# An expert layer's last turns reordered, and its results summed by selection products

## What is computed

```
logits = x @ w_router + b_router                 # 512 x 32
top_val, top_idx = top_k(logits, 4); gate = softmax(top_val)
for each token and each of its 4 experts e:
    hb = x @ w_e1[e] + b_e1[e]                   # 1024 -> 2048
    y += gate * (clamped_swiglu(hb) @ w_e2[e] + b_e2[e])   # 1024 -> 1024
out = layer_norm(DEEPNORM_ALPHA * x + y, ln2_g, ln2_b)
```

## Time and profile before

| | us |
|---|---|
| median of three runs | 1627.82 |
| the profiled execution | 1628.22 |
| its span | 1626.5 |
| TensorE busy | 1445.0 |
| VectorE busy | 605.8 |
| GpSimd busy | 348.2 |
| ScalarE busy | 141.2 |

### The profile page before, as it was taken

How to read it: one execution, slowest core, us unless ns; L and a number is a source line. 1 busy time by engine, 2 the same in 40 slices (tenths; PEclk the granted TensorE clock), 3 DMA queues, 4 the chain that set the end, 5 groups by cost and what they waited for, 6 DMA issues and landing times.

```text
span 1626.5 us, 28900 instructions
## 1 busy us (share of the span) xinstructions
PE 1445.0 (89%) x12008; PEld 638.0 (39%) x12009; DVE 605.8 (37%) x1048; ACT 141.2 (9%) x227; POOL 348.2 (21%) x390
## 2 busy tenths in 40 slices
PE   7999999999999979989977687897789999999855
PEld 6744444444444633333322232332233333344222
DVE  5034344210003645434433533443443354344326
ACT  4011322110000010000000000000000000000001
POOL 1060000000000022422332332332232233223225
PEclk9999999999999989999999999999999999999987
DMA  5522200163114389999999999999999999999936
GB/s 187 183 73 72 60 1 0 46 193 91 46 45 168 131 314 381 420 423 424 422 422 425 421 422 422 424 420 424 424 421 422 424 423 422 422 400 425 424 146 253
DMA packets 94327, 474.32 MB, mean 292 GB/s; under 512 B 15022, under 2 KB 60854, under 8 KB 68696
## 3 DMA queue, kind: packets, MB, share of 16 engines
q1 hardware_dynamic: 79520, 445.09, 67.8%
q0 software_dynamic: 12240, 16.86, 2.9%
q10 hardware_dynamic: 2536, 11.94, 1.9%
HBM read 469.59 MB, written 20.97 MB: 302 GB/s over the span
## 4 chain that ended last, share of the span: by engine, by line
PE 61%; DMA 31%; DVE 3%; issue 2%; ACT 1%; POOL 1%; SPq 0%; DVEq 0%; POOLq 0%
DMA big<-in_w_e 30%; PE ps L1543 19%; PE ps L1569 10%; PE ps L1397 7%; PE ps L1318 5%; PE ps L1279 4%; PE ps L1427 3%; PE ps L1455 3%; PE ps L1411 3%; PE ps L1405 1%; PE ps L1346 1%; PE ps L1364 1%; PE ps L1634 0%; DMA rest<-x_rows,P 0%; PE ps L1471 0%
## 5 line engine op out<-in xcount | busy, mean ns | idle before, releaser
L1543 PE MATMUL ps<-big,rest 128*32 128x512 f32 x5056 | 568.2, 599 | 95.8 <-DMA big<-in_w_e 82.2
L1543 PEld LDWEIGHTS ps<-big,rest 128*32 128x32 f32 x5056 | 159.9, 110 | 490.7 <-issue 490.4
L1569 PE MATMUL ps<-big,rest 128*32 128x256 f32 x5120 | 289.7, 383 | 32.1 <-DMA big<-in_w_e 30.9
L1569 PEld LDWEIGHTS ps<-big,rest 128*32 128x32 f32 x5120 | 167.0, 111 | 164.7 <-issue 42.8
L1155 DVE MEMSET stat<- 128x1 f32 x31 | 1.8, 59 | 493.0 <-PE ps L1543 493.0
L614 POOL DMA_INDIRECT rest<-x_rows,idx x124 | 152.4, 1229 | 58.3 <-issue 31.9
L626 POOL DMA_INDIRECT expert_rows<-rest,slot x128 | 126.9, 992 | 62.3 <-issue 34.1
L798 ACT ACTIVATE rest<-rest 128x1024 f32<-128x1024 f32 x32 | 33.9, 1060 | 924.6 <-DVE rest L1139 924.6
L610 POOL COPY idx<-P 128x4 uint32 (+1 forms) x31 | 5.8, 188 | 475.7 <-DVE rest L1156 468.1
L1318 PE MATMUL ps<-big,rest 128*128 128x512 f32 x192 | 84.4, 601 | 2.8 <-ACT big L676 2.8
L1156 DVE STREAM_TRANSPOSE rest<-rest 128x1024 f32<-128x1024 f32 x31 | 64.3, 2073 | 18.2 <-issue 18.2
(11 more groups left out here) (236 smaller groups left out, 1091.2 us busy)
## 6 DMA issues: line engine op xcount, KB each, us to landing
big<-in_w_e SPq DMA_DIRECT2D x190, 2048.0 KB, 25.5
rest<-in_w_in SPq DMA_DIRECT2D x14, 1024.0 KB, 5.2
big<-expert_rows ACTq DMA_DIRECT2D x8, 1024.0 KB, 12.1
gate_area<-in_w_in SPq DMA_DIRECT2D x8, 512.0 KB, 5.4
rest<-in_w_in SPq DMA_DIRECT2D x8, 512.0 KB, 4.7
big<-in_w_out SPq DMA_DIRECT2D x1, 4096.0 KB, 13.0
X<-in_x SPq DMA_DIRECT2D x4, 512.0 KB, 9.0
gate_area<-in_w_branch_mlstm SPq DMA_DIRECT2D x4, 512.0 KB, 6.3
```

The lines of the kernel that those rows point to most:

```text
L1543: last = mm(ps[TB * g:TB * (g + 1), b, :], xT[:, k, b, :], w1, start=(k == 0), stop=(k == KD - 1))
L1569: last = mm(ps[TB * g:TB * (g + 1), 4 + b // 2, YW * (b % 2):YW * (b % 2 + 1)], acts[:, k, b, :], W2[:, k, YW * g:YW * (g + 1)], start=(fi ...
```

## The change

SP, TensorE and VectorE end with fc2(31) ahead of fc1(32), and SP loads W2(31) ahead of W1(32). The rows of turns 1 to 31 are read back by SP's queue, in four loads of 2 MB and with 32 tokens x 4 choices on the 128 partitions, each into the place of one pair of W1. Those of turn 32 are not written to HBM: they stay in SBUF, are moved into one piece (`yL`, 16 copies of 32x256 on VectorE and ScalarE) and are added by a product with `slot_gate`, a matrix (row by token) that holds each row's gate where row and token belong together. Its row of gates is fetched by an indirect DMA from a copy of the gates in HBM (`gates`), and the places of these rows in `expert_rows` are set to zero at the start. The four choices of 32 tokens are summed by one product with `row_gate` (128 rows by 32 tokens); the gates for it come by a second copy in HBM (`main_gates`, zero for rows of turn 32), read back transposed (`main_rows`). The residual enters the sums by a product with the identity. The closing norm reads PSUM; GpSimd's and ScalarE's steps over rows are gone from it, and each tile is stored in two halves. `gates_of_late_rows` stands where the diagonals were made, and `late_selections` behind `turn_a(2)`, ahead of VectorE's loop.

```diff
+    gates_dram = nc.dram_tensor("gates", (S, TOPK), F32, kind="Internal").ap()
+    main_dram = nc.dram_tensor("main_gates", (S, TOPK), F32, kind="Internal").ap()
+    gate_of_row = gates_dram.rearrange("t (k a) -> (t k) a", a=1)
+    y_rows = y_dram.rearrange("t k n -> (t k) n")
...
+QROWS = TB * TOPK
+NQ = S // TB
+assert QROWS == P and NQ * D <= W1_COLS and 2 * FF * KD == NT * 4 * FF
+yg = cut(big, 0, NQ, D)
+row_gate = cut(gate_area, 0, NQ, TB)
+slot_gate = gate_area[:, 4 * S:5 * S]
+yL = cut(rest, SPARE_AT + KF * CAP, CG, YW)
...
-    with sp.Fori(1, n_it - 1) as it:
+    with sp.Fori(1, n_it - 2) as it:
         load_w1(it + 1, sp.snap((it + 1) % E))
         load_w2(it, sp.snap(it % E))
+    load_w2(n_it - 2, E - 2)
+    load_w1(n_it - 1, E - 1)
     load_w2(n_it - 1, E - 1)
+    sp.wait_ge(last_zeroed, 16 * NB)
+    sp.wait_ge(y_stored, n_it * (16 * NB) - 16 * NB)
     for i in range(NT):
-        sp.wait_ge(out_ready, i + 1)
-        sp.dma_start(out_rows[P * i:P * (i + 1), :], X0v[:, i, :]).then_inc(out_stored, 16)
-    sp.wait_ge(out_stored, 16 * NT)
+        sp.wait_ge(w1_used, n_it * PAIRS + (i + 1 - PAIRS))
+        sp.dma_start(yg[:, NT * i:NT * (i + 1), :],
+                     y_rows[TOPK * P * i:TOPK * P * (i + 1), :].rearrange("(j p) n -> p j n", p=P)).then_inc(yg_landed[i], 16)
+    for i in range(NT):
+        for n in range(D // BANK):
+            sp.wait_ge(out_ready, 2 * i + n + 1)
+            sp.dma_start(out_rows[P * i:P * (i + 1), BANK * n:BANK * (n + 1)], X0v[:, i, BANK * n:BANK * (n + 1)]).then_inc(out_stored, 16)
+    sp.wait_ge(out_stored, 32 * NT)
...
+    nc.gpsimd.tensor_copy(last_slot, slot_table[:, bass.ds(n_it * NB - NB, NB)]).then_inc(last_slots, 1)
+    pool.wait_ge(last_slots, 1)
+    own_wait()
+    for b in range(NB):
+        pool.indirect_dma_start(out=y_quarters, out_offset=bass.IndirectOffsetOnAxis(ap=last_slot[:, b:b + 1], axis=0),
+                                in_=no_rows, in_offset=None,
+                                bounds_check=S * TOPK * CG - 1, oob_is_err=False).then_inc(last_zeroed, 16)
+    pool.wait_ge(late_consts, 1)
+    pool.wait_ge(last_rows, 1)
+    pool.wait_ge(gates_stored, 32)
+    pool.indirect_dma_start(out=last_gate, out_offset=None, in_=gate_of_row,
+                            in_offset=bass.IndirectOffsetOnAxis(ap=last_row, axis=0),
+                            bounds_check=S * TOPK - 1, oob_is_err=False).then_inc(last_gates, 16)
...
     scatter(n_it - 1)
-    scatter(n_it)
-    pool.wait_ge(x1_scaled, 1)
-    pool.wait_ge(diags_ready, TOPK * NT)
-    def add_first(i):
-        pool.wait_ge(yg_front[i], 16)
-        row = yg[:, i, 0, :]
-        step(nc.gpsimd.tensor_scalar(row, row, gatew[:, TOPK * i:TOPK * i + 1], None, ALU.mult))
-        nc.gpsimd.tensor_tensor(X0v[:, i, :], X0v[:, i, :], row, ALU.add).then_inc(first_added, 1)
-    for i in range(NT):
-        add_first(i)
...
+    act.wait_ge(gates_ready, 1)
+    act.dma_start(gates_dram.rearrange("(i p) k -> p i k", p=P), cut(gatew, 0, NT, TOPK)).then_inc(gates_stored, 16)
+    act.dma_start(main_dram.rearrange("(i p) k -> p i k", p=P), cut(main_gate, 0, NT, TOPK)).then_inc(gates_stored, 16)
     act.wait_ge(x1_stored, 16 * NT)
     act.activation(X0[:], X0[:], ACT.Copy, scale=DEEP_ALPHA).then_inc(x1_scaled, 1)
+    act.wait_ge(gates_stored, 32)
+    act.dma_start(main_rows.rearrange("p (j a) -> p j a", a=1),
+                  main_dram.rearrange("(j t) (k a) -> (t k) j a", t=TB, a=1), allow_slow_non_contiguous=True).then_inc(main_landed, 16)
...
-    act.wait_ge(w2_used, n_it * W2_UNITS)
-    act.wait_ge(y_stored, n_it * (16 * NB))
-    for i in range(NT):
-        act.dma_start(yg[:, i, 0:2], y_dram[P * i:P * (i + 1), 0:2]).then_inc(yg_front[i], 16)
-        act.dma_start(yg[:, i, 2:4], y_dram[P * i:P * (i + 1), 2:4]).then_inc(yg_back[i], 16)
+    act.wait_ge(y_ready, n_it + 1)
+    for g in range(2, CG):
+        for b in range(NB):
+            act.activation(yL[TB * b:TB * (b + 1), g, :], yS[TB * g:TB * (g + 1), b, :], ACT.Copy).then_inc(late_moved, 1)
...
-        if i >= 1:
-            act.wait_ge(centred, i)
-            act.activation(X0v[:, i - 1, :], X0v[:, i - 1, :], ACT.Copy, scale=stat[:, s0 - 2:s0 - 1]).then_inc(scaled, 1)
...
+    def gates_of_late_rows():
+        step(nc.vector.tensor_scalar(last_round, cnt[:, E:E + 1], 1.0 / CAP, 0.5 * (CAP - 1) / CAP - 1.0, ALU.mult, ALU.add))
+        step(nc.vector.tensor_scalar(last_iter, last_round, float(E), float(E - 1), ALU.mult, ALU.add))
+        step(nc.vector.tensor_scalar(main_gate, itern[:], last_iter, None, ALU.not_equal))
+        nc.vector.tensor_tensor(main_gate, main_gate, gatew[:], ALU.mult).then_inc(gates_ready, 1)
+        dve.wait_ge(last_slots, 1)
...
+    def late_selections():
+        dve.wait_ge(late_consts, 1)
+        dve.wait_ge(main_landed, 16)
+        for j in range(NQ):
+            nc.vector.tensor_scalar(row_gate[:, j, :], fourth, main_rows[:, j:j + 1], None, ALU.mult).then_inc(row_gates, 1)
+        dve.wait_ge(last_rows, 1)
+        dve.wait_ge(last_gates, 16)
+        nc.vector.tensor_scalar(slot_gate, token_row, last_token, last_gate, ALU.is_equal, ALU.mult).then_inc(slot_gates, 1)
+    def move_late_rows(g):
+        for b in range(NB):
+            nc.vector.tensor_copy(yL[TB * b:TB * (b + 1), g, :], yS[TB * g:TB * (g + 1), b, :]).then_inc(late_moved, 1)
...
     turn_a(1)
-    for n in range(TOPK * NT):
-        i, k = n // TOPK, n % TOPK
-        nc.vector.tensor_scalar(gate_diag[:, n, :], ident[:], gw[:, i, k:k + 1], None, ALU.mult).then_inc(diags_ready, 1)
+    gates_of_late_rows()
     spread_b2(1)
     spread_b1(2)
     turn_x(3)
     swiglu(2)
     take_y(1, first=True)
     turn_a(2)
+    late_selections()
     with dve.Fori(2, n_it - 1) as it:
         spread_b1(it + 1)
         turn_x(it + 2)
...
         spread_b2(it)
         take_y(it)
         turn_a(it + 1)
+    spread_b2(n_it - 1)
+    take_y(n_it - 1)
     spread_b1(n_it)
     swiglu(n_it)
     turn_a(n_it, into=last_aT)
-    spread_b2(n_it - 1)
-    take_y(n_it - 1)
     spread_b2(n_it)
     take_y(n_it)
+    dve.wait_ge(y_ready, n_it + 1)
+    move_late_rows(0)
+    move_late_rows(1)
...
+    def norm_2_center(i):
         s0 = 16 * i
-        dve.wait_ge(first_added, i + 1)
+        b = SUM_AT[i]
+        dve.wait_ge(combined, i + 1)
         for n in range(D // BANK):
-            dve.wait_ge(combined, 2 * i + n + 1)
-            half = t[:, BANK * n:BANK * (n + 1)]
-            nc.vector.tensor_tensor(half, half, ps[:, 2 * i + n, :], ALU.add).then_inc(combined_read, 1)
-            dve.wait_ge(combined_read, 2 * i + n + 1)
-            piece_statistics(NORM2 + i, n, half)
+            piece_statistics(NORM2 + i, n, ps[:, b + n, :])
         step(nc.vector.bn_aggr(stat[:, s0 + 12:s0 + 14], stat[:, s0:s0 + 12]))
         nc.vector.tensor_scalar(stat[:, s0 + 13:s0 + 14], stat[:, s0 + 13:s0 + 14], LN_EPS, None, ALU.add).then_inc(var2_ready, 1)
-        layer_norm_center(NORM2 + i, t)
+        step(nc.vector.scalar_tensor_tensor(out=X0v[:, i, :], in0=ps[:, b:b + 2, :].rearrange("p b n -> p (b n)"),
+                                            scalar=stat[:, s0 + 12:s0 + 13], in1=gain[:], op0=ALU.subtract, op1=ALU.mult))
     def norm_2_root(i):
...
         step(nc.vector.scalar_tensor_tensor(out=q, in0=y, scalar=var, in1=y, op0=ALU.mult, op1=ALU.mult))
         step(nc.vector.tensor_scalar(q, q, -0.5, 1.5, ALU.mult, ALU.add))
         nc.vector.tensor_tensor(y, y, q, ALU.mult).then_inc(centred, 1)
-        return y
-    def norm_2_bias(i):
-        dve.wait_ge(scaled, i + 1)
-        nc.vector.tensor_tensor(X0v[:, i, :], X0v[:, i, :], bias[:], ALU.add).then_inc(out_ready, 1)
+        dve.wait_ge(centred, i + 1)
+        for n in range(D // BANK):
+            t = X0v[:, i, BANK * n:BANK * (n + 1)]
+            nc.vector.scalar_tensor_tensor(out=t, in0=t, scalar=y, in1=bias[:, BANK * n:BANK * (n + 1)], op0=ALU.mult, op1=ALU.add).then_inc(out_ready, 1)
     for i in range(NT):
-        norm_2_statistics(i)
-        y = norm_2_root(i)
-        if i >= 1:
-            norm_2_bias(i - 1)
-    dve.wait_ge(centred, NT)
-    nc.vector.scalar_tensor_tensor(out=X0v[:, NT - 1, :], in0=X0v[:, NT - 1, :], scalar=y, in1=bias[:],
-                                   op0=ALU.mult, op1=ALU.add).then_inc(out_ready, 1)
+        norm_2_center(i)
+        norm_2_root(i)
...
-    with pe.Fori(1, n_it) as it:
+    with pe.Fori(1, n_it - 1) as it:
         blocks1 = blocks_of(it)
         pe.wait_ge(xT_turned, it)
         pe.wait_ge(h_read, it)
...
         pe.wait_ge(aT_turned, it)
         pe.wait_ge(y_ready, it)
         fc2(it, blocks2)
-    last_blocks = blocks_of(n_it - 1)
+    fore_blocks, last_blocks = blocks_of(n_it - 2), blocks_of(n_it - 1)
+    pe.wait_ge(aT_turned, n_it - 1)
+    pe.wait_ge(y_ready, n_it - 1)
+    fc2(n_it - 1, fore_blocks)
+    pe.wait_ge(xT_turned, n_it - 1)
+    pe.wait_ge(h_read, n_it - 1)
```

(84 more changed lines are left out.)

14 lines of the change are left out of this document (8 added, 6 removed).

## The result

| | before | after |
|---|---|---|
| median | 1627.96 | 1644.77 |
| lowest to highest | 1625.74 to 1628.15 | 1643.08 to 1645.62 |
| profiled execution, span | 1628.22, 1626.5 | 1645.62, 1643.8 |

The change makes the kernel slower by 17 us (16.8 between the medians; ratio 1.0109, 95% interval 1.0096 to 1.0123, which is 17.7). I had said 1636, 8 us more than before. The direction and the mechanism of the stall were right, the size was half of it.

A forecast was written before the change was run, and what follows sets the result against it. The prediction took the weight stream to bound the expert loop, with an uncovered tail behind it. 1628.2 - 13.5 (tail) + 21 (stall) = 1635.7, about 1636 us; range 1617 to 1645, likeliest case 1629 to 1646.

The forecast's parts named there:

- What bounds the kernel: Expert loop: bound by its weight stream, DMA engines 90% busy or more; idle time there is not regained.
- The stall, +21: Loop start: VectorE waits for `main_rows`, its small packets alternating with weight packets; stream runs dry, 21 us late (17 to 27).
- Rival (a): `main_rows` load: sixteen elements form one packet, 8 turns, some 5 us, no stall; total 1618; chance 0.20.
- my step from long turns to a quick landing: `main_rows` load: if engines drain 9 to 17 descriptors per turn, some 10 turns and not 128.
- The small packets before the gap, "which swallows it": Loop start: small packets and 0.26 MB of zero rows cost 3 us of engine time, hidden by the stream's gap.
- Rival (c): Loop start: 4-byte writes cost four times 12.5 ns, gate stores caught; stall 27 us or more, 1645; 0.68 jointly with computed stall.
- The last turns in another order: Loop end: last weight no later (1 us either way), but fc2(32) waits for swiglu and turn, ending 4.3 us later.
- Rows loaded behind the last weight: Tail: four 2 MB loads queue behind W2(32) at 410 to 422 GB/s and end at 1590.8.
- The last expert's rows: Tail: copies take 3.3 us; products per tile 1.7 + 1.75 us, plus 2.5 for half pace after idling.
- The closing norm: Tail, VectorE: 4.9 us a tile in place of 6.17, then 3.0 us for the last store.
- The sum: Whole kernel: 1628.2 - 13.5 + 21 = 1635.7, about 1636 us.
- the tail: Behind the weight stream: new tail ends the span at 1613.0 in place of 1626.5, -13.5 us (-17 to -10).

The follow-up runs named there:

- experiment 1: Changed kernel with `main_rows` loaded as one 64-byte run per partition instead of 2048 4-byte pieces: 1624.05 us, ratio 0.9988 to the kernel before.
- experiment 3: Changed kernel with `late_selections` moved behind VectorE's loop, loads unchanged: 1641.85 us in one execution.
- experiment 5: Kernel before with only the two stores of the gates to HBM added, at the changed kernel's place: 1631.22 us, ratio 1.0026.
- experiment 6: Kernel before with only the other order of the last turns (SP, TensorE, VectorE), old tail kept: 1636.77 us, ratio 1.0060.
- experiment 7: Experiment 4 with the last turns put back in the order of before: 1610.13 us, ratio 0.9902 to the kernel before.
- experiment 2: Changed kernel with the load of 4-byte pieces issued twice and VectorE waiting for both: 1646.24 us in one execution.
- experiment 4: Changed kernel with gate operations, both gate stores and the 4-byte-piece load moved earlier, before the stream needs the engines: 1620.26 us, ratio 0.9968 to the kernel before.
- experiment 8: Experiment 4 plus twelve unused small products on TensorE while the last rows are copied: 1619.73 us, ratio 0.9955 to the kernel before.
- experiment 9: Changed kernel with the 4-byte-piece load of `main_rows` on SP's queue behind W1(3), not ScalarE's: 1628.04 us, ratio 1.0015 to the kernel before.
- experiment 10: Experiment 7 with copies split nine to VectorE, seven to ScalarE, and nine clock-keeping products on TensorE: 1607.35 us, ratio 0.9889 to the kernel before.

## Why the prediction was right in its direction and wrong in its size

**What bounds the kernel:** right. The stall passed one to one into the time (experiment 1), since the stream has no idle share.

**The stall, +21:** right as a mechanism and as a size; 20.3 by the trace of experiment 1, 19.7 by the times. The packets alternate one to one, the stream dries at 680 (I said 677), the load lands at 682.2 (678.5), TensorE resumes at 691.3 (687.0) and W1(5) is asked for at 699.8 (694.8). Each step stands 3 to 5 us later than I put it, because the whole started 3 us later, for the reason of the next point. The sum was made for one waiting engine; the second wait, for the bias behind the load on ScalarE's queue, changed nothing here, but would have made the fix "move the wait" fail (experiment 3). Rival (a), many elements to a packet, is out: each piece took a turn of its own. The Trainium skill ("DMA: Bandwidth & Descriptors", Queues, rings and completion order) has an engine drain a whole packet of typically 9 to 17 descriptors before it switches queues. This trace differs from it for loads of this form: with such turns the small pieces would come in groups of nine or more, and the ten windows of 0.1 us hold at most 6 of them, beside as many weight packets within one. The time to landing alone would not have told this, and my step from long turns to a quick landing was incomplete: I had let only the small load's turns grow. If the weights' turns were as long, the load would wait for as many weight packets in all.

**The small packets before the gap, "which swallows it":** this step failed. I had costed the stores of the gates as engine time, 3 us with the zero rows, and had put them into the cover of the stall. Their cost is not engine time: in the changed kernel the 2 MB loads behind them run at half the rate (216 GB/s for 426) for some 5 us, at the restart of the stream, 3.3 us in all (experiment 5, the stores alone: 4.2 us by the times, 2.1 in the trace). The stall doesn't hide it, as W1(3) lies ahead of the stall and sets where it begins. Rival (c) had the stores caught among the weights; what happened was the reverse. This is of the size of the 3.7 us between 24.7 and 21, which two single traces give and which is no better known than to some 2 us.

**The last turns in another order:** this step failed in its size. I had it as 4.3 us of delay for fc2(32); alone it costs 10 (experiment 6) and in the new tail 10.7 (experiment 7). The turn behind the last first product was read rightly: 8.5 us. fc1(32) ended 1.8 us later than I said (1590.1, 33.7 behind the second product of turn 30; I had 31.9), behind a gap of 2.04 us with "issue" as its reason ahead of its second pair; and fc2(32) took 11.9 us in place of 7.4. I had taken both halves at full clock because the `residual` products fill the wait. They do, until 1597.0, and the first half does run at full clock. Then TensorE stands for 2.53 us with "issue" as its reason, while both halves' weights are there, and starts again at half clock (0.50 from 1605 to 1608). A packet of the queue "instruction" starts between 1602 and 1603, beside the loads of the rows that keep the engines at a share of 1.0. All seven kernels with the new tail and the new order (the changed one and experiments 1 to 4, 8 and 9) have this gap of 2.5 us in the same place, with row loads beside it, and in each such a packet starts within 0.2 us of TensorE's stop. Experiments 6, 7 and 10 have no gap there; in 6 no row loads run, and in 7 and 10 they start only in the last 3 us of the product, though instruction packets pass beside it. I take the gap for instructions that are fetched beside those loads, but this was argued, not tried; the kernel before has one such gap too, of 1.22 us, up to 629.5 beside the weights.

**Rows loaded behind the last weight:** right; issued at 1588.4 to 1597.5, 401 to 410 GB/s, never last until experiment 10. It doesn't need the reorder, though (experiment 7), which I hadn't asked.

**The last expert's rows:** copies of 3.5 us for eight on ScalarE (I had 3.3), late products at half pace 3.51 (1.7 and 2.5). Right within 1 us; the half pace is the clock (experiment 8).

**The closing norm:** 5.05 us a tile for 4.9, and 2.5 for 3.0 at the end. Right.

**The sum.** Predicted: 21 - 13.5 = 7.5. Measured in the profiled executions: 24.7 - 7.3 = 17.4. Of the 9.9 between them 3.7 lie in the stream, and 6.2 in the tail, which are the reorder's two terms within 0.1 (1.8 for fc1(32), 4.5 for fc2(32)). The measured 1644.8 still lies inside the stated range, at its edge (1645), and that is luck: the edge was rival (c)'s, whose 4-byte packets at four times 12.5 ns did not come (9.9 to 10.5 ns), and the 6 us that the tail fell short by stood in no term or rival. Without the reorder's term (4.3) my tail was -17.8; experiment 7, which has the tail without the reorder, gave -16.6 us by its median and -19.3 in its trace (75.4 us behind the mark, in place of 94.7).

## What to carry to other kernels

Beside a stream of large packets, count a small transfer in packets and not in bytes: each costs one packet time of the stream, and all that is issued on the same queue behind it waits as well. Put such loads where the stream is idle, or on the stream's own queue, in whole runs if the layout lets you, and cost the loads that come behind a burst of tiny HBM writes too. Before bringing a store forward by turning two products round, ask what stands between the last weight and the last product: work that was hidden beside the last loads (here the swiglu and the turn, 8.5 us) comes to lie on the path, and if the early store was not last it buys nothing.

## What was not expected of the hardware

- 1024 writes of 16 bytes to HBM (16 KB) just ahead of a restarting stream cost 4.2 us (2.4 to 5.9; 2.1 in the one trace), seen as 3 to 13 packets of weights a microsecond in place of 25, each of 1.7 us in place of 0.61 in one microsecond of it. What holds them is not shown.
- An issue on a queue that holds 2048 pieces takes 21.8 to 39.2 us beside the weights (ScalarE), and SP's two issues of W2 behind such pieces 13.8 us.
- Pieces of 4 bytes pass at 9.9 to 10.5 ns where nothing shares the turns, whether the engines had run dry or the weights stood in the same queue.
- TensorE stood 2.5 us for no releaser, in the same place in seven kernels, while the DMA engines were full with row loads and a packet of the instruction queue started; in the three kernels with no row loads beside most of that product it didn't. The cause is not shown.
